# Expert blocks: the first two slabs of the third matrix split into high and low parts too, the low parts by POOL

## The reference, cut to what matters

```python
y = jnp.zeros_like(t)
for e in range(N_EXPERTS):
    h = jax.nn.silu(t @ w_gate[e]) * (t @ w_up[e])      # 1024 -> 512
    y = y + combine[:, e:e + 1] * (h @ w_down[e])       # 512 -> 1024
```

## Time and profile before

| | us |
|---|---|
| median of three runs | 2906.59 |
| lowest and highest | 2905.07, 2906.65 |
| profiled execution: span from first to last instruction (no other time of it is given) | 2917.2 |
| busy in the span: PE, PE's weight loads | 2792.7, 2557.6 |
| busy in the span: DVE, ACT, POOL | 1784.1, 1102.0, 373.8 |
| mean granted clock of PE | 0.976 |

### The profile page before, as it was taken

How to read it: one execution, slowest core, us unless ns; L and a number is a source line. 1 busy time by engine, 2 the same in 40 slices (tenths; PEclk the granted TensorE clock), 3 DMA queues, 4 the chain that set the end, 5 groups by cost and what they waited for, 6 DMA issues and landing times. The chain is left out here.

```text
span 2917.2 us, 57947 instructions
## 1 busy us (share of the span) xinstructions
PE 2792.7 (96%) x25303; PEld 2557.6 (88%) x25303; DVE 1784.1 (61%) x2702; ACT 1102.0 (38%) x1783; POOL 373.8 (13%) x223
## 2 busy tenths in 40 slices
PE   8999999999999999999999999999998999899997
PEld 7988898898999998998999899999885887778784
DVE  5633335554888645733335555888626985677886
ACT  6221324533333225322324533333324343366664
POOL 0210122121111000310122120111000000000001
PEclk9999999999999999999999999999999998799998
DMA  4211222265444342211222162333332311199996
GB/s 139 77 39 36 71 80 69 64 211 187 129 132 131 117 144 84 77 46 36 68 77 75 65 210 82 128 131 131 116 94 67 97 40 65 67 411 397 389 389 244
DMA packets 115350, 380.15 MB, mean 130 GB/s; under 512 B 12800, under 2 KB 13968, under 8 KB 114704
## 3 DMA queue, kind: packets, MB, share of 16 engines
q1 hardware_dynamic: 89712, 307.18, 31.2%
q10 hardware_dynamic: 17712, 41.36, 4.0%
q0 software_dynamic: 7664, 27.82, 2.5%
HBM read 340.17 MB, written 36.13 MB: 129 GB/s over the span
## 5 line engine op out<-in xcount | busy, mean ns | idle before, releaser
L307 PE MATMUL PS<-HR,HIGHR 128*128 128x264 f32 (+1 forms) x3008 | 857.8, 285 | 0.0
L307 PE MATMUL PS<-XR,HIGHR 128*128 128x264 f32 (+2 forms) x1792 | 564.0, 315 | 17.1 <-DVE HR L431 7.8
L307 PEld LDWEIGHTS PS<-HR,HIGHR 128*128 128x128 f32 x3008 | 571.7, 190 | 2.9
L307 PE MATMUL PS<-XR,RINGR 128*128 128x264 f32 (+1 forms) x1600 | 456.9, 286 | 0.0
L307 PE MATMUL PS<-HH,HIGHR 128*128 128x264 f32 (+2 forms) x1504 | 437.1, 291 | 10.6 <-ACT SMALL L388 5.7
L291 ACT CAST HIGHR<-RING 128x1024 fp32r<-128x1024 f32 (+2 forms) x340 | 330.7, 977 | 270.5 <-DMA RING<-wts 108.1
L307 PE MATMUL PS<-HH,RINGR 128*128 128x264 f32 (+2 forms) x1504 | 432.3, 287 | 0.0
L307 PE MATMUL PS<-ARENA 64*64 64x64 f32 (+7 forms) x8632 | 392.9, 235 | 18.9 <-issue 7.0
L302 DVE TENSOR_TENSOR RINGR<-RING,HIGHR 128x1024 fp32r<-128x1024 f32 (+2 forms) x272 | 305.3, 1126 | 153.8 <-ACT HIGHR L291 141.2
L307 PEld LDWEIGHTS PS<-ARENA 64*64 64x64 f32 (+4 forms) x8632 | 347.9, 140 | 53.0 <-issue 10.0
L307 PEld LDWEIGHTS PS<-XR,HIGHR 128*128 128x128 f32 x1792 | 340.6, 190 | 46.2 <-issue 15.7
(11 more groups left out here) (388 smaller groups left out, 4785.1 us busy)
## 6 DMA issues: line engine op xcount, KB each, us to landing
RING<-wts SPq DMA_DIRECT2D x324, 512.0 KB, 3.7
ARENA<-wmoe SPq DMA_DIRECT2D x210, 512.0 KB, 7.2
RING<-wts SPq DMA_DIRECT2D x52, 256.0 KB, 2.9
gates<-STAGE ACTq DMA_DIRECT2D x48, 264.0 KB, 4.2
ARENA<-gates ACTq DMA_DIRECT2D x48, 264.0 KB, 3.1
ys<-RING ACTq DMA_DIRECT2D x17, 512.0 KB, 6.8
ys<-STAGE POOLq DMA_DIRECT2D x15, 512.0 KB, 11.4
RING<-wts SPq DMA_DIRECT2D x16, 384.0 KB, 3.0
```

Of the source, the lines that this page charges most:

```text
L307: return e.matmul(out, lhsT, rhs, start=start, stop=stop, skip_group_check=True)
```

## The change

It makes slabs g+8 and g+9 like the others of the block. ACT also casts their high parts, into two places more (HY and HXG), between g+7 and g+10. POOL subtracts to get their low parts, on top of the raw slabs; for this it has a semaphore of its own, `moe_pool`, and `expert_low` takes the semaphore's name. `down(0)` and `down(1)` are `mm3` like the rest. The product's turned halves both become pairs: HTH and HTL are twice as large, HT2 goes, ACT casts both halves, and DVE subtracts both (`turned(0)`, `turned(1)`), the first between product(0) and product(1).

```diff
@@ -232,7 +232,7 @@
 ARENA_R = {"ML": (6336, 8 * T), "MH": (13200, 8 * T), "FL": (0, NFF * T), "FH": (NFF * T, 18 * T),
            "UL": (22000, 2176), "PH": (4224, 2112), "BL": (0, 4224), "BH": (17424, 4224),
            "OL": (16504, 2048), "QL": (0, 2048), "GH": (2048, 4096), "HH": (29600 - 8 * T, 8 * T), "UH": (22648, 4096),
-           "HX": (3976, 1024), "WR": (5000, 24576)}
+           "HX": (3976, 1024), "HY": (2952, 1024), "WR": (5000, 24576)}
 
 
 class Kernel:
@@ -2729,7 +2729,7 @@
 
 
     i = g % 12
-    return k.WL[:, g % NRAW], k.WR[:, g % NRAW], k.WR[:, NRAW + i] if i < 8 else k.HX[i - 10] if i >= 10 else None
+    return k.WL[:, g % NRAW], k.WR[:, g % NRAW], k.WR[:, NRAW + i] if i < 8 else k.HX[i - 8]
 
 
 def expert_high(k, e, w, *which):
@@ -2740,6 +2740,12 @@
             w.wait_ge(*k.s[f"expert{g % NRAW}"][g])
             if g >= 12:
                 w.wait_ge(*k.s["moe_pe"]["slab", g - 12])
+            elif g == 8:
+                w.wait_ge(*k.s["route_dve"]["index"])
+                w.wait_ge(*k.s["moe_pe"][0, "rows", 1])
+            elif g == 9:
+                w.wait_ge(*k.s["u_out"][3])
+                w.wait_ge(*k.s["moe_pe"][0, "rows", 1])
             elif g == 10:
                 w.wait_ge(*k.s["u_out"][3])
             elif g == 11:
@@ -2747,13 +2753,13 @@
             e.copy(high, raw).then_inc(*k.s["moe_act"].done(("high", g)))
 
 
-def expert_low(k, e, w, *which):
+def expert_low(k, e, w, *which, by="moe_dve"):
 
     for g in which:
         if g < 12 * NB:
             raw, low, high = expert_slab(k, g)
             w.wait_ge(*k.s["moe_act"]["high", g])
-            e.tensor_tensor(low, raw, high.bitcast(F32), SUB).then_inc(*k.s["moe_dve"].done(("low", g)))
+            e.tensor_tensor(low, raw, high.bitcast(F32), SUB).then_inc(*k.s[by].done(("low", g)))
 
 
 def turn_pe(k, e, w, bk):
@@ -2831,25 +2837,18 @@
             q = 2 * half + i
             ins = e.transpose(k.PS[:, b, 128 * i:128 * i + 128], k.HB[:, 128 * q:128 * q + 128], k.c("id"))
         ins.then_inc(*P.done((bk, "turned", half)))
-        banks.emptied_by(b, 1, "moe_dve" if half else "moe_act", (bk, "turned", half))
+        banks.emptied_by(b, 1, "moe_dve", (bk, "turned", half))
 
     def down(q):
         if q == 0:
             banks.place(w, ("down2", bk), 2)
             banks.emptied_by(banks.at["down2", bk], 2, "moe_dve", (bk, "out"))
         raw, low, high = expert_slab(k, g + 8 + q)
-        if q < 2:
-            w.wait_ge(*s["moe_act"][bk, "turned", 0])
-            w.wait_ge(*s[f"expert{(g + 8 + q) % NRAW}"][g + 8 + q])
-        else:
-            w.wait_ge(*V[bk, "turned", 1])
-            w.wait_ge(*V["low", g + 8 + q])
+        w.wait_ge(*V[bk, "turned", q // 2])
+        w.wait_ge(*(s["moe_pool"] if q < 2 else V)["low", g + 8 + q])
         for half in range(2):
             out, c = k.PS[:, banks.at["down2", bk] + half, :], slice(512 * half, 512 * half + 512)
-            if q < 2:
-                ins = mm(e, out, k.HT2[:, q, :], raw[:, c], q == 0, False)
-            else:
-                ins = mm3(e, out, (k.HTH[:, q - 2], k.HTL[:, q - 2]), (high[:, c], low[:, c]), False, q == 3)
+            ins = mm3(e, out, (k.HTH[:, q], k.HTL[:, q]), (high[:, c], low[:, c]), q == 0, q == 3)
         ins.then_inc(*P.done(("slab", g + 8 + q)))
 
     for i in range(4):
@@ -2874,11 +2873,10 @@
         if bk:
             w.wait_ge(*P["slab", g - 1])
         w.wait_ge(*P[bk, "turned", half])
-        e.copy(k.HTH if half else k.HT2,
-               k.PS[:, at["product", bk, half], 0:256].rearrange("p (k t) -> p k t", k=2)).then_inc(
+        e.copy(k.HTH[:, 2 * half:2 * half + 2], k.PS[:, at["product", bk, half], 0:256].rearrange("p (k t) -> p k t", k=2)).then_inc(
             *A.done((bk, "turned", half)))
 
-    expert_high(k, e, w, g + 6, g + 7, g + 10, g + 11)
+    expert_high(k, e, w, *range(g + 6, g + 12))
     if bk:
         w.wait_ge(*V[bk - 1, "product", 1])
     w.wait_ge(*P["slab", g + 3])
@@ -2909,12 +2907,14 @@
         e.tensor_tensor(k.HB[:, cols], k.PS[:, at["up2", bk, half], 0:256], k.SI[:, cols], MUL).then_inc(
             *V.done((bk, "product", half)))
 
-    def turned():
-        at_product = k.PS[:, at["product", bk, 1], 0:256].rearrange("p (k t) -> p k t", k=2)
+    def turned(half):
+        at_product = k.PS[:, at["product", bk, half], 0:256].rearrange("p (k t) -> p k t", k=2)
+        part = slice(2 * half, 2 * half + 2)
         if bk:
             w.wait_ge(*P["slab", g - 1])
-        w.wait_ge(*A[bk, "turned", 1])
-        e.tensor_tensor(k.HTL, at_product, k.HTH.bitcast(F32), SUB).then_inc(*V.done((bk, "turned", 1)))
+        w.wait_ge(*A[bk, "turned", half])
+        e.tensor_tensor(k.HTL[:, part], at_product, k.HTH[:, part].bitcast(F32), SUB).then_inc(
+            *V.done((bk, "turned", half)))
 
     w.wait_ge(*s["row_d"]["g2"])
     expert_low(k, e, w, g + 6, g + 7, g + 10, g + 11)
@@ -2923,9 +2923,10 @@
     expert_low(k, e, w, g + 12)
     product(0)
     expert_low(k, e, w, g + 13)
+    turned(0)
     product(1)
     expert_low(k, e, w, g + 14)
-    turned()
+    turned(1)
     expert_low(k, e, w, g + 15, g + 16, g + 17)
     if bk >= 2:
         w.wait_ge(*s[f"result{bk % 2}"][bk - 2])
@@ -2949,6 +2950,7 @@
                 *k.s["row_c"].done(name))
     if bk + 1 < NB:
         fetch_rows(k, e, w, bk + 1)
+    expert_low(k, e, w, 12 * bk + 8, 12 * bk + 9, by="moe_pool")
 
 
 def fetch_slabs(k, e, w, bk, which):
@@ -3236,7 +3238,7 @@
         ffn_pool(k, e, w, l)
     mixer_pool(k, e, w)
     w.wait_ge(*s["route_dve"]["tokens"])
-    blocks(k, e, w, None, block_pool)
+    blocks(k, e, w, "moe_pool", block_pool)
     combine_pool(k, e, w)
 
 
@@ -3282,7 +3284,7 @@
            "out_dve", "up_pe", "down_pe", "down_dve", "ffn_act", "ffn_dve", "ffn_pool", "ada_pe", "ada_dve", "ln_pe",
            "ln_act", "ln_dve", "in2_pe", "in2_act", "in2_dve", "conv_dve", "hgrn_pe", "hgrn_act", "hgrn_dve",
            "row_pe", "row_dve", "out2_pe", "out2_dve", "route_pe", "route_act", "route_dve", "moe_pe", "moe_act",
-           "moe_dve", "sum_dve", "sum_pe")
+           "moe_dve", "moe_pool", "sum_dve", "sum_pe")
 TRANSFERS = ("load", "one", "cols", "x0", "x1", "x2", "x3", "gate_out0", "gate_out1", "regate0", "regate1", "regate2", "zero_results", "kept",
              "reload", "row_mod", "row_a", "row_b", "row_c", "row_d", "u_out", "gather0", "gather1", "gather2", "gather3",
              "rows", "result0", "result1", "out",
@@ -3432,9 +3434,8 @@
     k.UB = [[tiles(UBR[:, 2048 * i + 1024 * x:2048 * i + 1024 * x + 1024]) for x in range(2)] for i in range(2)]
     k.HB, k.SI = ring[:, 7168:7680], ring[:, 8704:9216]
     k.unit = k.SI[:, 0:128]
-    k.HT2 = tiles(ring[:, 7680:7936], 2)
-    k.HTH, k.HTL = [tiles(at(name, F32R, rg + a, 256), 2) for name, a in (("HTH", 7936), ("HTL", 8192))]
-    k.HX = [at("HXH", F32R, 8 * T + 3072, 1024), parts["HX"]]
+    k.HTH, k.HTL = [tiles(at(name, F32R, rg + a, 512), 4) for name, a in (("HTH", 7680), ("HTL", 8192))]
+    k.HX = [parts["HY"], at("HXG", F32R, 8 * T + 2048, 1024), at("HXH", F32R, 8 * T + 3072, 1024), parts["HX"]]
 
     dram = lambda name, shape: nc.dram_tensor(name, shape, F32).ap()
     k.gates, k.xkeep = dram("gates", [48, 128, T]), dram("xkeep", [128, 8 * T])
```

## The result

| | before | changed |
|---|---|---|
| median of four runs, us | 2906.62 | 3002.61 |
| lowest and highest | 2905.07, 2913.24 | 2991.88, 3005.43 |
| profiled execution: own time, span | (not given), 2917.2 | 2991.88, 2990.1 |
| busy in the span: PE, DVE, ACT, POOL | 2792.7, 1784.1, 1102.0, 373.8 | 2803.1, 1844.0, 1134.2, 477.9 |
| first to last output of the stage, 16 block periods | 300.85 | 385.02 |

The changed kernel is slower, by a ratio of 1.0318 (1.0297 to 1.0339). The last line of the table is the measure that I use most: from the start of DVE's first output row (SCALAR_TENSOR_TENSOR from PS, ARENA, STAGE) to that of the seventeenth. Up to the experts all kernels here run the same instructions, but not in the same time in every execution.

A forecast was written before the change was run, and what follows sets the result against it. The prediction took PE to set the pace, with the head of each block on ACT and DVE already on its path. It summed 2906.6 + 58 (delay at full clock) + 26 (lowered clock) = 2990 us, range 2940 to 3010.

The forecast's parts named there:

- The saving on PE: In down(0) and down(1), six fp32r matmuls replace two f32 ones: 0.32 us saved each, 0.64 per block.
- ACT's casts: At the block's head, two more casts make the inputs of DVE's last two low parts ready later, at 5.35 and 6.30.
- rival C: At the block's head, POOL's low parts run beside DVE's; only ACT's two casts delay product(0), by 1.6: 2919 us, chance 0.08.
- The exclusion: At the block's head, POOL's and DVE's two-SBUF-input operations exclude each other whole; longest waiter goes next; POOL holds 2.2 us.
- product(0): On DVE, starts at 12.76 instead of 8.36, 4.4 us late; PE waits 4.1, in branched blocks 4.35.
- The stage at full clock: Expert stage: 3.46 us longer in seven blocks, 3.71 in nine, 58 us in all.
- The gather: POOL's fetch of the next rows comes at about 9.5 instead of 5, some 16 us before PE transposes them.
- The clock: On PE behind each block's idle gap, a lowered clock costs 1.64 us per block, 26 in all.
- rival B: In the expert stage, the same delays but PE's clock is not lowered: 2965 us, chance 0.14.
- D: At the block's head, DVE keeps the place when both want it: 2945 us, up to 2971 with half clocks, chance 0.10.
- F: Whole program: the change does its work but both effects cancel within 0.2%, between C and E, chance 0.03.
- E: Expert stage: product(0) stays inside its slack and PE's saving arrives whole, 11 us, so 2896, chance 0.05.

The follow-up runs named there:

- the repetition: Changed kernel and the kernel before timed once more, both as they are: 2993.71 us against 2912.03, ratio 1.0259.
- the matmuls alone: Changed kernel without POOL's low parts and ACT's casts of g+8 and g+9; down(0), down(1) read another slab's high part: 2899.14 us.
- the gap filled: Changed kernel with 17 useless matmuls on PE ahead of its wait for product(0): 2969.55 us.
- the changed order: Changed kernel, all low parts on DVE, only g+6 to g+9 ahead of product(0) on ACT and DVE, last two low parts behind the output: 2900.93 us.
- the order alone: Kernel before, with product(0) ahead of the low part of g+12 and the last two low parts behind the output: 2907.35 us.

## Why the prediction was right

2990 was forecast, 3002.61 and in the repetition 2993.71 measured, both inside 2940 to 3010. The mechanism is the one that was put on record, and the runs show each part of it by itself. The steps one by one:

- **The saving on PE**, 0.64 per block: 0.60 by the matmuls alone.
- **ACT's casts.** The two more were to delay product(0) by 1.6 (rival C); it was 1.53 with the low parts left out.
- **The exclusion** and who goes next. DVE's two low parts were to end 7.09 and 10.43 behind the output; they ended 7.19 and 10.55. POOL's place, taken as 2.2 us, fits within 0.1.
- **product(0)** at 12.76: measured 12.81, in the branched blocks 12.97. PE's gap, 4.1 and 4.35: measured 3.97 and 4.14, in part since the record of its transposes follows the end of DVE's product by 0.05, not 0.12.
- **The stage at full clock**, 58: with the gap filled, 359.68 − 300.85 = 58.8. Per block 3.55 and 3.75, for 3.46 and 3.71.
- **The gather** behind POOL's two low parts, at about 9.5: it starts at 2678.83, 9.61 behind the output, and PE waited for no rows (its only wait between 2560 and 2960 is the one shown).
- **The clock**, 26: measured 25.3, which refutes rival B. The estimate came from one gap of 3.31 us with other work behind it, 44 operations in place of 12 up and 6 down matmuls. That it met the mean of 1.58 so closely is in part luck: single blocks lost from 1.3 to 2.5.
- **The sum for the stage**, 84: measured 84.2 and 83.1. The table's 96 is 12 more. No step of the change in the traces accounts for them, and they are within the spread ahead of the stage: the medians of before stand between 2906.62 and 2912.45 in these comparisons, those of the changed kernel at 2993.71 and 3002.61. The executions behind those medians have no trace but the profiled ones, so that the 12 are this spread is likely, not shown.

What of the forecast was wrong is small. Block 0 was called even, and it is: from the first matmul of the experts to its output it took 24.18 and 24.01 in before's traces, 24.09 and 24.11 in the changed kernel's. The next two periods took 24.96 and 24.52 (24.47 and 23.84 in the repetition), where the five behind them took 23.83 to 23.85 (forecast: 18.755 + 3.46 + 1.64 = 23.86). The stretch of the earlier trace rows is ten times 18.755 and not quite ten periods, which took 188.34: the one into the first branched block takes 19.48. PE's only idle time in it, 0.52, is a wait for product(0) there, so in that block the slack was already gone:

```profile
2723.53 0.44 PE L2832 MATMUL PS<-CST,RING 128*128 128x128 f32 x2 [0.53 <-DVE RING L2909]
```

And "two SBUF inputs" is narrower than what the trace of before shows. In the stretch of the earlier trace rows DVE also has an operation with one tensor from SBUF, the other operand being a column of COLS:

```profile
72.56 2.02 DVE L711 TENSOR_SCALAR ARENA<-ARENA,COLS 128x528 f32<-128x528 f32 x1
```

It began while POOL worked (71.50 to 74.28) and took 2.02; the shortest of its kind took 0.48. In the expert stage all of DVE's operations that met POOL's had two inputs from SBUF or read PS, so the forecast did not depend on it.

The rivals. C fell by the durations of HXH and HX; the kernel without the low parts shows what C would have cost, 2924.62 for the 2919 forecast, or 13.0 above its own before for the 12.4 forecast. D (DVE keeps the place) did not occur, since POOL went first in each of the 16 blocks behind the first, and no experiment made it real. F, two effects that cancel, would have needed a time within 0.2% of before. E, PE's whole saving, is what the changed order gave: 16 periods in 289.96, 10.9 less than before, for the 0.64 × 16 = 10.2 counted; 0.7 of it is the wait at the first branched block, which the order alone takes away.

Where the 84 us go, then, follows from the chain of kernels, each with one part more. Matmuls alone −9.6; ACT's casts +21.1 (312.35 − 291.21); the exclusion at full clock +47.3 (359.68 − 312.35); the clock +25.3. That they add up to 84.2 is no evidence, as each is the difference of neighbours; but the delays bear them out: product(0) comes 12.81 − 9.89 = 2.92 later by the exclusion, 16 × 2.92 = 46.7. Not tried: a wait order in which DVE takes its place ahead of POOL by semaphore, and other numbers of pieces.

## What to carry to other kernels

Work that is moved to an idle engine is free only if neither the making of its inputs nor its turn at what it shares with another engine stands ahead of the operation that the bound engine waits for: look from the bound engine's next wait backwards, and put there only what that wait needs. Here the same instructions cost 84 us in one order and gained 10 in another. GpSimd's two-input operations cost nothing beside VectorE work that read PSUM, and 47 us beside work that read SBUF. And an idle stretch of about 4 us on TensorE cost another 1.6 behind it, through the clock, so a forecast of such a gap needs two terms.

## What the runs showed that I had not expected

- Short gaps lower the clock sometimes. With the low parts on DVE, fifteen blocks kept it behind gaps of 1.74 to 2.80 us, and one did not, behind a gap of 2.01. PE's transposes of product(0) and product(1) in three blocks:

```profile
2735.99 0.44 PE L2838 MATMUL PS<-CST,RING 128*128 128x128 f32 x2 [2.80 <-DVE RING L2907]
...
2739.08 0.38 PE L2838 MATMUL PS<-CST,RING 128*128 128x128 f32 x2
...
2857.97 0.44 PE L2838 MATMUL PS<-CST,RING 128*128 128x128 f32 x2 [2.01 <-DVE RING L2907]
...
2861.05 0.38 PE L2838 MATMUL PS<-CST,RING 128*128 128x128 f32 x2
...
2878.30 0.69 PE L2838 MATMUL PS<-CST,RING 128*128 128x128 f32 x2 [2.01 <-DVE RING L2907]
...
2882.90 0.38 PE L2838 MATMUL PS<-CST,RING 128*128 128x128 f32 x2
```

The first two pairs lie 3.09 and 3.08 apart, at a granted clock of 1.00; the third lies 4.60 apart, at 0.63, behind the same gap of 2.01 as the second. With POOL in pieces, the clock fell in four blocks, behind gaps of 2.00, 2.25, 2.25 and 2.59, and stayed in the twelve others, one of them behind a gap of 3.03; the four then took 21.85 to 22.14 us, most others 20.5 to 20.7. Behind each of the changed kernel's gaps, 3.89 to 4.94, it fell. So the length of the gap alone doesn't decide it between 2.0 and 3.0, and what does is open.

- The price behind a gap is not fixed. In the first full block of the changed kernel 5.60 us ran at a granted clock of 0.50 (1.2 of 2.4 GHz) throughout; later 4.60 us at 0.63 did the same work (columns as in the windows above):

```profile
2585.40:2591.00 5.60, 5.60 (x21) 4.91 (x22) 3.01 (x4) 1.32 (x2) 0.00 (x0) 0.50 1.01 398
2682.50:2687.10 4.60, 4.60 (x20) 4.05 (x21) 2.96 (x4) 1.32 (x2) 0.00 (x0) 0.63 0.84 269
```

At full clock it takes 3.08, so the gap cost 2.5 and 1.55.

- A POOL instruction in four pieces is not four quarters: HY's four took 4.09 us where the whole took 2.67, HXG's 5.75 for 3.39. The shortest piece took 0.72, so four of them come to 2.9 where a whole one undisturbed took 2.38; the pieces that met DVE took up to 1.74, about 1.0 more, a little less than a DVE low part (1.13).
